# Recurrent and mixture-of-experts blocks on one core: loads, squares, a row table and the last norm placed elsewhere

## What is computed

```python
hx = modulate(rmsnorm(x, norm1_g), sh1, sc1)        # tokens
hc = modulate(rmsnorm(ctx, norm1_g), sh1c, sc1c)    # 256 context tokens
attn_x = latent_window_attention(qx, kx, vx, kc, vc, attn_sink)
x = x + g1 * (concat([attn_x, pool_x]) @ w_out)
hx2 = modulate(rmsnorm(x, norm2_g), sh2, sc2)
scores = sigmoid(hx2 @ w_router)                    # 64 experts, top 8 of each token
y_rows = expert_of_block(hx2[row_tok]) * row_w      # blocks of 128 rows, one expert each
shared = (silu(hx2 @ ws_gate) * (hx2 @ ws_up)) @ ws_down
x = x + g2 * (sum of the token's 8 rows + shared)
return rmsnorm(x, final_g)
```

## Time and profile before

| | us |
|---|---|
| three runs | 4949.12, 4917.72, 4923.84 |
| median | 4923.84 |
| the profiled execution | 4947.87 |
| its span, first to last instruction | 4946.1 |
| TensorE busy in it | 4184.1 (85%) |
| VectorE, ScalarE, GpSimd busy | 1721.6, 1108.8, 762.4 |
| mean granted TensorE clock | 0.911 of 2.4 GHz |

### The profile page before, as it was taken

One profiled execution on the slowest core, in us unless ns is written; L12 is line 12 of the kernel. 1 busy time (PEld: TensorE's weight loads), 2 busy tenths in 40 slices (PEclk: granted clock), 3 DMA queues, 4 the chain that ended last, 5 costly groups with the idle time before them and its releaser, 6 DMA issues. The chain is left out here.

```text
span 4946.1 us, 73793 instructions
## 1 busy us (share of the span) xinstructions
PE 4184.1 (85%) x28560; PEld 2783.5 (56%) x28560; DVE 1721.6 (35%) x2452; ACT 1108.8 (22%) x1499; POOL 762.4 (15%) x555
## 2 busy tenths in 40 slices
PE   6999668879996998578889978889759999999962
PEld 3887656656665886466756654544524444444431
DVE  3554754442412004655524221730401111111127
ACT  1111433321212112433312231620101111111110
POOL 2221010012222220000023210000141010101114
PEclk8999878889998998788989999999779999999985
DMA  5663132412212222110022211010129999999966
GB/s 200 213 191 124 66 119 92 164 44 76 91 62 77 93 93 83 38 41 28 7 81 81 82 38 36 1 40 31 64 86 337 353 363 354 361 358 356 360 250 249
DMA packets 241858, 715.29 MB, mean 145 GB/s; under 512 B 26977, under 2 KB 110690, under 8 KB 205794
## 3 DMA queue, kind: packets, MB, share of 16 engines
q1 hardware_dynamic: 191490, 536.83, 31.2%
q10 hardware_dynamic: 25632, 93.33, 4.7%
q0 software_dynamic: 24512, 81.84, 4.6%
HBM read 584.95 MB, written 126.98 MB: 144 GB/s over the span
## 5 line engine op out<-in xcount | busy, mean ns | idle before, releaser
L434 PE MATMUL ps<-s_proj_hS,s_proj_wS 128*128 128x512 f32 x3216 | 769.2, 402 | 62.5 <-POOL s_proj_wS L324 62.5
L434 PEld LDWEIGHTS ps<-s_proj_hS,s_proj_wS 128*128 128x128 f32 x3216 | 615.4, 192 | 212.3 <-ACT s_proj_wS L384 63.3
L1840 PE MATMUL ps<-s_mix_hS,s_mix_wS 128*128 128x512 f32 x1536 | 394.1, 412 | 40.8 <-POOL s_mix_wS L1699 35.5
L1840 PEld LDWEIGHTS ps<-s_mix_hS,s_mix_wS 128*128 128x128 f32 x1536 | 291.0, 190 | 135.8 <-issue 68.0
L2754 PE MATMUL ps<-s_exp_gu,keep_hT 128*128 128x512 f32 x736 | 340.1, 605 | 17.0 <-DMA s_exp_gu<-in_w_gu_dram 15.1
L2738 PE MATMUL ps<-s_exp_wd,s_exp_aT 128*128 128x512 f32 x736 | 332.8, 595 | 1.9 <-ACT s_exp_aT L2664 1.9
L2759 PE MATMUL ps<-s_exp_gu,keep_hT 128*128 128x512 f32 x736 | 330.9, 592 | 0.6 <-DMA s_exp_gu<-in_w_gu_dram 0.6
L1699 POOL TENSOR_TENSOR s_mix_wS<-s_mix_w,s_mix_wS 128x1024 fp32r<-128x1024 f32 x96 | 230.3, 2399 | 581.4 <-ACT s_mix_wS L1708 581.4
L2704 DVE TENSOR_TENSOR s_exp_sg<-s_exp_sg,ps 128x256 f32<-128x256 f32 x92 | 38.8, 421 | 663.0 <-ACT s_exp_sg L2685 663.0
L324 POOL TENSOR_TENSOR s_proj_wS<-s_proj_w,s_proj_wS 128x1024 fp32r<-128x1024 f32 x67 | 176.4, 2635 | 562.9 <-ACT s_proj_wS L384 562.9
L352 DVE COPY s_proj_o<-ps 128x512 f32<-128x512 f32 x66 | 45.5, 690 | 564.1 <-PE ps L434 564.1
(11 more groups left out here) (431 smaller groups left out, 5983.4 us busy)
## 6 DMA issues: line engine op xcount, KB each, us to landing
s_exp_gu<-in_w_gu_dram SPq DMA_DIRECT2D x184, 1024.0 KB
s_exp_wd<-in_w_down_dram SPq DMA_DIRECT2D x92, 1024.0 KB, 9.0
yrow<-keep_hT ACTq DMA_DIRECT2D x92, 512.0 KB
keep_mix<-in_w_ada_dram SPq DMA_DIRECT2D x80, 512.0 KB, 5.5
s_proj_w<-in_w_in_dram SPq DMA_DIRECT2D x66, 512.0 KB
proj<-s_proj_o ACTq DMA_DIRECT2D x66, 512.0 KB, 2.7
yrow<-keep_xT SPq DMA_DIRECT2D x4, 8192.0 KB
s_mix_w<-in_w_in_dram SPq DMA_DIRECT2D x64, 512.0 KB
```

What stands on the lines that cost most here:

```text
L434: mm = pe.matmul(k.ps[:, 6 + half if last else 2 * b + half, :], wS[:, b, x, t, :], hS[:, y, t, half * HALF:(half + 1) * HALF], start=(t = ...
L1840: mm = pe.matmul(k.ps[:, bank, :], wS[:, b, u, x, :], src[:, v, x, :], start=(x == 0 and u + v == 0), stop=(x == KT - 1 and u == 1))
```

## The change

1. The block that loads `ctxT` is gone; `ctxT`, both halves of `wkv` and then the gains are sent at the start of the first norm. Its squares of the context wait for `ctxT`; attention gets `wkv` ready.
2. In the attention slots TensorE issues the value products before the transposes.
3. In `project_out` ScalarE squares each finished tile, VectorE adds up the squares, and two products (4 instructions) give the sums; the second norm starts with Ln.
4. In `route` the logits wait for `w_router` alone. TensorE's order is logits, transposes, gate and up of f = 0, ranks, gate and up of f = 1, row table, down. The row table is made on the chip: a slot is 128 x (its row) + (its block); for each of 8 token tiles VectorE makes 8 one-hot tiles of the block (one instruction of 1024 columns) and 8 of the row times the token number (8 instructions of 128 columns), two tiles ahead at most, and TensorE multiplies them, 8 products of 128 columns, into one bank. The zero table, the 64 scatters and the way back are gone. The expert of each block now comes ahead of the gates, which come last.
5. In `experts` SyncE waits, in the first block only, for the gathered rows before it issues the second half of the weights and all that follows.
6. In `combine` each tile of 128 tokens gets its own square, sum, Ln and Exp, a multiplication by the deviation on VectorE (one instruction of 1024 columns), 8 multiplications by the gain on ScalarE, and an output DMA of 1024 runs of 512 B; for the last tile VectorE does both in 8 instructions of 128 columns. VectorE takes tile i-2 after it has added tile i-1 to `xT`.

```diff
 def rms_modulated
+            for dst, src, landed in loads:
+                sp.dma_start(dst, src).then_inc(landed, 16)
             sp.dma_start(gain[:], I["norm_g"]).then_inc(ld, 16)
...
 def attention, TensorE
                 if t < NU:
                     scores(t)
+                if t - LAG_V >= 0 and (t - LAG_V) % 2:
+                    values((t - LAG_V) // 2)
                 if 0 <= t - LAG_T < NU:
                     turned(t - LAG_T)
-                if t - LAG_V >= 0 and (t - LAG_V) % 2:
-                    values((t - LAG_V) // 2)
...
 def project_out
+            pe.wait_ge(added, KT - 1)
+            for half in range(2):
+                pe.matmul(k.ps[:, 6 + half, :], k.ones[:], total[:, half * HALF:(half + 1) * HALF], start=True, stop=True)
+                act.activation(sq[:, j % 2] if j else total[:], k.xT[:, j], ACT.Square).then_inc(sq_ready, 1)
+                dve.tensor_tensor(total[:], total[:], sq[:, j % 2], ALU.add).then_inc(added, 1)
...
 def route, VectorE
+            for i in range(NTT):
+                wait(dve, hot_done, i - 1)
+                dve.tensor_tensor(atblk[:, i % 2], iota[:].unsqueeze(1).to_broadcast([P, TOPK, P]),
+                                  placef[:, 1, i].unsqueeze(2).to_broadcast([P, TOPK, P]), ALU.is_equal).then_inc(hot_ready, 1)
+                for j in range(TOPK):
+                    ins = dve.tensor_scalar(atrow[:, i % 2, j], iota[:], placef[:, 0, i, j:j + 1], tokf[:, i:i + 1], ALU.is_equal, ALU.mult)
+                ins.then_inc(hot_ready, 1)
...
+            shared(1)
+            dve.wait_ge(hot_done, NTT)
+            mine.mark(dve.tensor_copy(k.idx[:], k.ps[:, 1, 0:NBLK]))
...
 def route, TensorE
-            pe.wait_ge(ld_c, 96)
+            pe.wait_ge(ld_wr, 16)
...
+            gate_up(0)
...
+            pe.wait_ge(act_ready, 1)
+            gate_up(1)
+            for i in range(NTT):
+                pe.wait_ge(hot_ready, 2 * i + 2)
+                for j in range(TOPK):
+                    mm = pe.matmul(k.ps[:, 1, 0:NBLK], atrow[:, i % 2, j], atblk[:, i % 2, j],
+                                   start=(i == 0 and j == 0), stop=(i == NTT - 1 and j == TOPK - 1))
+                mm.then_inc(hot_done, 1)
...
 def experts, SyncE
                     sp.dma_start(gu[:, u, 0:KH], I["w_gu"][e, :, 0:KH]).then_inc(ld_ga[u], 16)
+                    if isinstance(b, int) and b == 0:
+                        sp.wait_ge(ld_x[0], 16)
...
 def combine
+                sp.dma_start(k.out[:, :, tile(i)].rearrange("j p t -> p j t"), o[:, i % 2]).then_inc(st_o[i % 2], 16)
...
+            def deviation(i):
+                act.wait_ge(x_ready, i + 1)
+                wait(act, ss_ready, i - 1)
+                act.activation(sq[:, i % 2], k.xT[:, :, tile(i)], ACT.Square).then_inc(sq_ready, 1)
+                act.wait_ge(ss_ready, i + 1)
+                wait(act, n_ready, i - 1)
+                mine.do(act.activation(rstd[:, i % 2], k.ps[:, 4 + i % 2, 0:P], ACT.Ln, scale=1.0 / D, bias=EPS))
+                act.activation(rstd[:, i % 2], rstd[:, i % 2], ACT.Exp, scale=-0.5).then_inc(rstd_ready, 1)
...
+            for i in range(NTT):
+                deviation(i)
+                if i:
+                    gained(i - 1)
```

More of the change, by code:

```diff
@@ L1899, with rms_modulated @@
 C2 = 2 * NADA1
-def rms_modulated(k, name, jobs):
+def rms_modulated(k, name, jobs, loads=(), needs=(), sums=None):
     nc, I = k.nc, k.I
@@ L1920, in _ @@
             mine = Steps(act, own_a)
-            for i, (src, dst, N, g, c, v) in enumerate(jobs):
+            for i, (src, dst, N, g, c, v) in enumerate(jobs if sums is None else ()):
+                if i < len(needs) and needs[i] is not None:
+                    act.wait_ge(needs[i], 16)
                 for j in range(KT):
@@ L2410, in _ @@
             sp.dma_start(k.eb[:], ebd.rearrange("p o -> o p")).then_inc(ld_back, 16)
[L2411 to L2423, removed]
-            pool.wait_ge(st_slot, 16 * NTT * TOPK)
+            sp.wait_ge(ld_back, 16)
         @block.scalar
@@ L2560, in _, with gate_up @@
                 tr.then_inc(h_ready, 1)
+            pe.wait_ge(h_taken, NTT)
+            pe.wait_ge(ld_s, 16)
+            def gate_up(f):
+                for m in range(2):
+                    for half in range(2):
+                        for t in range(KT):
+                            mm = pe.matmul(k.ps[:, 2 + 2 * m + half, :], wgu[:, m, f, t, :],
+                                           k.hT2[:, t, half * HALF:(half + 1) * HALF], start=(t == 0), stop=(t == KT - 1))
+                    mm.then_inc((g_ready, u_ready)[m], 1)
+            gate_up(0)
+            pe.wait_ge(ld_c, 80)
             pe.wait_ge(mask_ready, 1)
@@ L2820, in _, with sums @@
                     to_residual(i - 1)
+                if i >= 2:
+                    scaled(i - 2)
             to_residual(NTT - 1)
-            dve.wait_ge(ld_g, 16)
-            dve.wait_ge(rstd_ready, 1)
-            dve.wait_ge(x_ready, NTT)
-            for j in range(KT):
-                dve.scalar_tensor_tensor(k.hT2[:, j], k.xT[:, j], fg[:, j:j + 1], rstd[:], ALU.mult, ALU.mult).then_inc(o_ready, 1)
+            scaled(NTT - 2)
+            scaled(NTT - 1)
         @block.tensor
         def _(pe):
+            def sums(i):
+                pe.wait_ge(sq_ready, i + 1)
+                wait(pe, rstd_ready, i - 1)
+                for t in range(KT):
+                    mm = pe.matmul(k.ps[:, 4 + i % 2, 0:P], k.ones[:], sq[:, i % 2, t], start=(t == 0), stop=(t == KT - 1))
+                mm.then_inc(ss_ready, 1)
             for i in range(NTT):
@@ L2875, in program @@
             ctxT, hcT = s.sb("ctxT", [P, KT, CTX]), s.sb("hcT", [P, KT, CTX])
-            ld = s.sem("ld")
-            with nc.Block() as block:
-                @block.sync
-                def _(sp):
-                    sp.dma_start(ctxT[:], I["ctxT"]).then_inc(ld, 16)
-                    sp.wait_ge(ld, 16)
-            rms_modulated(k, "norm1", [(k.xT, k.hT2, T, 0, C2, 1), (ctxT, hcT, CTX, 0, C2, 2)])
-            attention(k, hcT)
+            wkv = s.sb("wkv", [P, 2, KT, P])
+            ld, ld_kv = s.sem("ld"), s.sem("ld_kv")
+            rms_modulated(k, "norm1", [(k.xT, k.hT2, T, 0, C2, 1), (ctxT, hcT, CTX, 0, C2, 2)],
+                          loads=((ctxT[:], I["ctxT"], ld), (wkv[:, 0], I["w_in2"][W2K], ld_kv), (wkv[:, 1], I["w_in2"][W2V], ld_kv)),
+                          needs=(None, ld))
+            attention(k, hcT, wkv, ld_kv)
         pooling(k)
         project_out(k)
-        rms_modulated(k, "norm2", [(k.xT, k.hT2, T, 1, C2 + 3 * KT, 1)])
+        rms_modulated(k, "norm2", [(k.xT, k.hT2, T, 1, C2 + 3 * KT, 1)], sums=6)
         route(k)
```

149 lines of the change are left out of this document (88 added, 61 removed).

## The result

The kernel after takes 4895.06 us (median of 11 runs, 4889.12 to 4914.01), the kernel before, run beside it, 4923.11 (4902.85 to 4949.12): ratio 0.9948, 95% interval 0.9933 to 0.9963. Two of the 63 runs of the kernel before that stand beside the experiments took 6672.65 and 6378.58 us at a mean granted clock of 0.61 and 0.65, and the ratios leave them out. The profiled execution of the kernel after took 4896.57 us (span 4894.8). The traces are compared by milestones: the time from each to the next, worked out from the start of the row that marks it (for the value product and the last copy, from its end). The last column is a further execution of the kernel before (b0, in the first experiment).

The account below looks back on a forecast made before the run. TensorE sets the experts' pace with DMA close behind; the rest is seams, with VectorE and DMA nearly full in the last stage. Terms 5.2 + 5.1 - 5.6 + 9.3 + 16.7 + 4 + 5 = 39.7; 4947.9 - 39.7 = 4908, range 4876 to 4922.

Parts of the forecast that it names:

- the stall: Routing: 25.7 us unaccounted for before a shared-expert multiplication; comes in some executions, costs 27 us, goes with the scatters.
- first norm, attention's start: Squares start when `ctxT` is sent, 5.2 us gained; attention's first product comes sooner, 5.1 us gained.
- attention loop: Value products wait for the output copy, 0.33 us in 14 pairs, plus 1.0 at the end: -5.6, bounds -8 and 0.
- output projection, second norm, logits' loads: Second norm starts sooner after the last output tile, 9.3 us gained; logits wait for fewer loads, some 1.7.
- routing: Routing stage: TensorE carries everything in a row; 16.7 us gained with the logits' 1.7, bounds 12 and 20.
- start of the experts: Weights held back, so gathered rows come 8.0 us behind the last copy, not 12.1: 4 us gained, bounds 0 and 6.
- last stage: Tile-by-tile norm shortens the end by 6 us, taken as 5 because output writes share with gathers; bounds -4 and 12.
- Rival 1: Routing's unexplained gap is in every execution, so all 39.7 come off fast runs too: 4883; chance 0.24.
- Rival 2: Attention loop falls to the lower clock behind the longer gap: 87 us lost, 4995; chance 0.04.
- The 1.0 at the loop's end: Attention loop's end: the second of the last two transposes waits for a ScalarE copy, 1.0 us more lost.
- the tile of 2.75 us: Routing's row table: VectorE's time per tile, 1.22 plus eight instructions of 0.19; range 2.3 to 3.4.
- rival 3: Row table and last stage cost their upper bounds, 3.4 a tile (+4) and gathers pushed back (+9): 4921; chance 0.15.

Follow-up runs that it names:

- b0: Kernel before, unedited, profiled once more: 4921.86 us, ratio 1.0008 to the kernel before.
- e2: Kernel after without SyncE's wait for the gathered rows in the experts' first block: 4901.65 us, ratio 0.9970 to the kernel before.
- b1: Kernel before, unedited, profiled again on the third chip: 4958.81 us.
- e1: Kernel after with TensorE's old order in the attention slots (transposes ahead of value products): 4887.27 us, ratio 0.9945 to the kernel before.
- e8: Kernel after with early attention copies, row table inside second gate and up, and TensorE's old slot order: 4919.83 us, ratio 0.9944 to the kernel before.
- e7: Kernel after with the ranks put back ahead of the first gate and up: 4912.35 us, ratio 0.9971 to the kernel before.

## Why the prediction was right or wrong

That the kernel would stay within 1%, and the range, were right. The range says little: 46 us wide, it ends 1 us below the time before. The size was not right: against its own figure of 4921 for an execution without the stall the forecast was a gain of 13 us, and 28 were measured (4923.11 less 4895.06). Most terms held in mechanism; the one that missed by most is routing.

| term | predicted | measured, against the trace of before |
|---|---|---|
| first norm, attention's start | 10.3 | 11.2 |
| attention to the first scores | none | 1.2 |
| attention loop | -5.6 | -8.8 (-12.1 in four further traces) |
| output projection, second norm, logits' loads | 11.0 | 10.7 |
| routing (without the 1.7 of the logits) | 15.0 | 26.4 |
| start of the experts | 4 | 2.6; with routing 5.9 against b0 |
| experts | 0 | 0.6 |
| last stage | 5 | 7.3 |

**The stall.** Right that it does not belong to the kernel's own chain, as b0 shows, and that it is gone with the change. "Something that comes in some executions" is neither confirmed nor refuted: on the third chip it seems to come in all. The argument for it, that "the 27 us fit the spread" of the three runs, is weak, since the unedited part alone differs by 11 us among the four traces of the kernel before. Its price was mis-sized, 27 for 23.0. In b0 the last scatter ends 158.1 us behind the first logits, 1.7 later than in the trace of before. And from that end (3643.4) to the experts' first load (3652.4) it is 9.0 us, of which 2.4 follow the stage's end (3677.04 to 3679.44 before), so the way back took 6.6 and not the 4.4 that took the stage to 3650. Rival 1 (all of 39.7 gained on every run, 4883) falls, since b0 has no stall.

**First norm, second norm.** Right in mechanism and size. The sums ran at the lower clock as assumed.

**Attention loop.** Right that the new order loses, and that it loses 0.33 a pair (10.68 against 10.34). The term left out what a gap of 1.94 does to the clock. Rival 2 asked whether a gap of this size is enough; the answer is sometimes. Behind gaps of 1.94 to 2.16 us one of the ten whole value products took over 5 us instead of 3.70 here, and four of ten in e2. Gaps of 1.61 never did it, one of 1.83 did in b1, the one of 2.40 in e1 did not, and those of 2.4 to 2.9 in e8 mostly did. The prediction gave the rival an all-or-nothing price of 87 us; against the kernel before, whose last whole value product is at the lower clock too (4.27 us), it is rather 3 to 7 us on top of the forecast 5.6. The 1.0 at the loop's end was right (1.16).

**Routing.** The order of what is late next was right: the scatters gone, TensorE carries everything, with the table at VectorE's pace. Three terms were mis-sized. The ranks were carried over at "18.7" though the new place has 512-column products ahead of them: 9.8, a miss of 8.9. The "2.9 for a cold start" of the first gate and up was not there. e7 confirms both (9.0 and 2.3). Against that, the tile of 2.75 us took 3.19: a 128-column `tensor_scalar` costs 0.27 (2.13/8), the upper of the two rows the estimate lay between. From the first table product to the down products it took 24.4 us (3583.03 to 3607.45), where the prediction had 20.3 and 1.4. The last row copy came 1.6 sooner behind the logits than before (43.3 for 44.9), which the prediction did not count. 8.9 + 2.9 - 2.7 + 1.6 = 10.7 of the 11.4 by which the term was off. The gain of 26.4 is for the most part the 23.0 of the stall: over an execution without it, routing with the start of the experts gains 5.9, where the prediction had a loss of 10 for routing and 4 back behind it.

**Start of the experts.** 2.7 (e2) instead of 4: the gathered rows came 9.5 us behind the copy instead of 8.0.

**Last stage.** The tail was right: predicted 21.9 us from the last tile in `xT` to the end, measured 21.1. The 1 us taken off for gathers pushed back, and rival 3's 9, did not come: up to the last tile the stage became 5.7 us longer, where the prediction's own steps give 6.1. A tile takes 14.12 us instead of 12.98, which VectorE's additional 1.22 accounts for, and DMA share and GB/s stand at 0.93 and 333 against 0.92 and 325 in the earlier trace rows. On the least transfer at line rate that the Trainium skill gives ("DMA: Bandwidth & Descriptors", Specifications): the 512 B writes show no loss here, so the trace does not speak against it.

## What to carry to other kernels

A duration carries to another place only with the clock it was measured at: ask what TensorE does just ahead of the new place. A wait made visible by a reordering names its cure: the copy that stands last in its engine's list although its input is long there. And where one trace has a gap that no engine's work accounts for, take a second trace of the same kernel, on another chip too, before any price hangs on it.

## What the runs showed of the hardware that was not expected

- The same 88 instructions with 64 columns took 18.7 and 18.8 us at a granted clock of 0.50 behind transposes, short idle times and the logits, and 9.8 us at 1.00 behind 27.7 us of 512-column products (2.4 GHz against 1.2).
- A gap of 1.94 to 2.16 us in an otherwise identical loop let the clock fall in a part of the pairs only, and in different numbers from one execution to the next (1, 3 or 4 of ten whole value products in five traces).
- In three of four traces of the kernel before, while the 64 small scatters run, VectorE's multiplication starts 25.8 to 31.5 us after the products that it needs, and ScalarE's copies are late too. The scatters themselves are no slower (83.1 to 83.3 us from the first start to the last, against 84.3 in the trace without the stall).
- The unedited first 2935 us vary by 32 us between executions; in the trace with 2914.41 the stretch 600 to 1200 us has granted clocks of 0.88 and 0.87, in that with 2946.19 it has 0.85 and 0.83.
